# Splitting the move of a transposed attention tile between ScalarE and VectorE in the last five units of layer 1

## The reference

```python
proj = rmsnorm(x) @ b_w_in                        # queries: 36 dilated heads and 4 memory heads of 64
mix = dilated_mixture(rope(q_dil), shared_k, shared_v)   # 3 (window, dilation) groups, combined
mo = memory_attention(q_mem, mem_k, mem_v)        # 256 memory tokens
x = x + concatenate([mix, mo]) @ w_out
x = x + peer(rmsnorm(x), ...)                     # 16 experts for each of 8 heads and 512 tokens
```

## Time and profile before

| | us |
|---|---|
| median of 3 runs | 3196.49 (3196.42 to 3196.59) |
| the profiled execution, its own time | 3195.37 |
| its span in the trace | 3193.6 |
| TensorE busy | 3150.6 |
| VectorE busy | 2545.1 |
| ScalarE busy | 1636.8 |

### The profile page before, as it was taken

The page is one execution under the profiler, slowest core; times in us unless marked ns, Lnnn a source line. Parts: engine busy times, 40 slices in busy tenths (PEclk is TensorE's granted clock), DMA queues, the critical chain, the costliest instruction groups (busy, mean ns, idle before and its releaser), DMA issues.

```text
span 3193.6 us, 48756 instructions
## 1 busy us (share of the span) xinstructions
PE 3150.6 (99%) x17822; PEld 2817.2 (88%) x17822; DVE 2545.1 (80%) x5378; ACT 1636.8 (51%) x3053; POOL 1020.8 (32%) x626
## 2 busy tenths in 40 slices
PE   8999999999999999999999989999999999999999
PEld 7878899999998888888978868899999998888887
DVE  5685898989857988885378876898989866888886
ACT  5343249696943333335255654248686853333333
POOL 1001464545422444520000000354445432444440
PEclk9999999999999999999999999999999999999999
DMA  5123269898999999993222214259898998999994
GB/s 199 44 66 118 85 222 349 308 351 303 354 366 340 379 391 390 396 367 115 68 86 74 87 61 138 81 171 337 314 346 312 345 383 315 374 401 398 389 392 146
DMA packets 324925, 827.33 MB, mean 259 GB/s; under 512 B 26064, under 2 KB 158672, under 8 KB 317520
## 3 DMA queue, kind: packets, MB, share of 16 engines
q1 hardware_dynamic: 250960, 555.75, 48.5%
q0 software_dynamic: 73728, 268.47, 22.5%
HBM read 718.16 MB, written 105.96 MB: 258 GB/s over the span
## 4 chain that ended last, share of the span: by engine, by line
PE 43%; DVE 3%; DMA 2%; ACT 1%; issue 1%; SPq 0%; DVEq 0%; ACTq 0%
PE p_bank L2346 16%; PE p1r_h_ps L2282 16%; PE ba_bank L416 6%; PE o_bank L1753 1%; DMA hiddens<-p_h_sb 1%; PE p1r_gate_ps L2330 1%; PE ba_oT_ps L476 1%; PE ba_t_ps L497 1%; PE p1r_s_ps L2306 0%; PE ba_s_ps L439 0%; DVE p_grow L2711 0%; DVE ba_e L644 0%; ACT p1r_cols L2452 0%; PE ba_s_ps L444 0%; DMA raw<-in_u 0%
## 5 line engine op out<-in xcount | busy, mean ns | idle before, releaser
L2413 ACT ACTIVATE peer_hi<-raw 128x1024 fp32r<-128x1024 f32 x540 | 570.9, 1057 | 673.9 <-PE p_bank L2346 604.3
L2703 DVE TENSOR_TENSOR peer_lo<-raw,peer_hi 128x1024 fp32r<-128x1024 f32 x434 | 530.0, 1223 | 308.1 <-ACT peer_hi L2413 307.3
L2244 POOL TENSOR_TENSOR peer_lo<-raw,peer_hi 128x1024 fp32r<-128x1024 f32 x106 | 263.3, 2485 | 1083.2 <-ACT peer_hi L2413 1083.1
L2256 POOL DMA_INDIRECT p_grow<-in_v_rows,p_expert x256 | 388.6, 1518 | 468.9 <-DVE p_acc L2720 384.1
L2256 POOL DMA_INDIRECT p_grow<-in_u_rows,p_expert x256 | 359.2, 1403 | 506.8 <-DVE p_hid L2711 479.2
L2346 PE MATMUL p_bank<-peer_hi,p_w_hi 128*128 128x512 f32 x1500 | 461.8, 389 | 0.0
L2346 PE MATMUL p_bank<-peer_hi,p_w_lo 128*128 128x512 f32 x1500 | 461.8, 389 | 0.0
L2346 PE MATMUL p_bank<-peer_lo,p_w_hi 128*128 128x512 f32 x1500 | 461.7, 389 | 0.0
L2282 PE MATMUL p1r_h_ps<-h_hi,peer_hi 128*128 128x384 f32 (+2 forms) x1152 | 396.9, 345 | 1.3 <-ACT p_h_sb L2431 0.9
L2282 PE MATMUL p0r_h_ps<-h_hi,peer_hi 128*128 128x384 f32 (+2 forms) x1152 | 396.7, 344 | 0.6 <-DVE peer_lo L2703 0.5
L2282 PE MATMUL p1r_h_ps<-h_lo,peer_hi 128*128 128x384 f32 (+2 forms) x1152 | 391.4, 340 | 0.0
(11 more groups left out here) (438 smaller groups left out, 5531.9 us busy)
## 6 DMA issues: line engine op xcount, KB each, us to landing
raw<-in_u SPq DMA_DIRECT2D x256, 512.0 KB, 6.1
raw<-in_v SPq DMA_DIRECT2D x256, 512.0 KB, 8.3
p_g_sb<-gates SPq DMA_DIRECT2D x64, 768.0 KB, 11.1
hiddens<-p_h_sb SPq DMA_DIRECT2D x240, 192.0 KB, 4.7
p_w_raw<-hiddens SPq DMA_DIRECT2D x60, 768.0 KB, 7.5
gates<-x SPq DMA_DIRECT2D x24, 1024.0 KB, 9.7
raw<-in_w_b_mix SPq DMA_DIRECT2D x38, 512.0 KB, 3.5
raw<-in_w_peer_q SPq DMA_DIRECT2D x32, 512.0 KB, 3.6
```

Source lines behind the costliest of these rows:

```text
L2244: pool.tensor_tensor(lo[:, m % NH, :], raw[:, m % NR, :], hi[:, m % NH, :].bitcast(F32), ALU.subtract).then_inc(lo_pool, 1)
L2256: pool.indirect_dma_start(out=grow[:, g % RG, :], out_offset=None, in_=table, in_offset=bass.IndirectOffsetOnAxis(ap=expert[:, at:at + 1], ...
L2413: act.activation(hi[:, n % NH, :], raw[:, n % NR, :], ACT.Copy).then_inc(hi_ready, 1)
L2703: dve.tensor_tensor(lo[:, m % NH, :], raw[:, m % NR, :], hi[:, m % NH, :].bitcast(F32), ALU.subtract).then_inc(lo_dve, 1)
```

## The change

For the units after 22, that is 23 to 27, `move_turned` on ScalarE moves only the first bank of `t_ps` (128x512). A new function `move_other` on VectorE moves the second. VectorE issues it in step s = n + 1, behind `finish(s-4)` and ahead of `maximum(s+1)` and of what else the step holds. A new semaphore, `t_moved_too`, counts it. `output(n)` and `turn(n)` on TensorE wait for both semaphores.

```diff
@@ output(n), TensorE
                 pe.wait_ge(t_moved, n + 1)
+                if n > DENSE:
+                    pe.wait_ge(t_moved_too, n - DENSE)
@@ turn(n), TensorE
                     pe.wait_ge(t_moved, n)
+                    if n - 1 > DENSE:
+                        pe.wait_ge(t_moved_too, n - 1 - DENSE)
@@ move_turned(n), ScalarE
-                act.activation(eT[:, n % 2, :, :], t_ps[:, :, :], ACT.Copy).then_inc(t_moved, 1)
+                b = slice(0, 1 if n > DENSE else 2)
+                act.activation(eT[:, n % 2, b, :], t_ps[:, b, :], ACT.Copy).then_inc(t_moved, 1)
@@ new, VectorE
+            def move_other(n):
+                dve.wait_ge(turned, n + 1)
+                dve.wait_ge(valued, n - 1)
+                dve.tensor_copy(eT[:, n % 2, 1, :], t_ps[:, 1, :]).then_inc(t_moved_too, 1)
@@ the loop over steps, VectorE
+                if DENSE < s - 1 < UNITS:
+                    move_other(s - 1)
                 if DENSE < s + 1 < UNITS:
                     maximum(s + 1)
```

More of the change, by code:

```diff
@@ L340, in dilated_stage @@
         (hi_ready, lo_ready, summed, bank_free, shuffled, sin_ready, rot_done, scored, maxed, biased, exped, turned,
-         t_moved, valued, copied, returned, inverted, o_moved, near_stored, near_loaded, shifted, cexped, combined, own,
+         t_moved, t_moved_too, valued, copied, returned, inverted, o_moved, near_stored, near_loaded, shifted, cexped, combined, own,
          mem_k_loaded, mem_v_loaded) = [
             st.sem(s) for s in ("hi_ready", "lo_ready", "summed", "bank_free", "shuffled", "sin_ready", "rot_done",
-                                "scored", "maxed", "biased", "exped", "turned", "t_moved", "valued", "copied",
+                                "scored", "maxed", "biased", "exped", "turned", "t_moved", "t_moved_too", "valued", "copied",
                                 "returned", "inverted", "o_moved", "near_stored", "near_loaded", "shifted", "cexped", "combined", "own",
```

## The result

The changed kernel takes 3209.94 us at the median of 5 runs (3205.37 to 3214.97), against 3196.42 for the kernel before in the same comparison. The ratio is 1.0039, with a 95% interval of 1.0029 to 1.0050, so some 9 to 16 us are lost. The forecast was 3208.3, in a range of 3204.0 to 3212.5.

A forecast was written before the change was run, and what follows sets the result against it. TensorE, busy 3150.6 of 3193.6 us, was taken as the bound. Queue delay 8.25 plus clock falls 2.0 and 1.6 made 11.85 us, added to 3196.49 for 3208.3 us, range 3204 to 3212.5.

The forecast's parts named there:

- Unit 23: VectorE's half delays maximum(25) and finish(21) by 1.61 us, so turn_back(22) starts 0.86 late.
- Units 24 and 25: The loop from turn to turn takes 5.29 us instead of 4.67, making turn(26) 2.10 late.
- Step 27: VectorE's shift waits behind move_other(26); ScalarE's combine(4) comes 5.27 us late and output(26) 4.82 late.
- Step 28: Combination waits behind VectorE's last half; turn_back(26) 7.23 us late, the output projection's first product 8.25 late, kept to the end.
- The clock: TensorE's clock falls to 1.2 GHz at two new long gaps, costing 2.0 and 1.6 us.
- the first fall: Half clock behind the gap before output(26), slowing output(26), turn_back(25) and turn(27); 2.0 us.
- A: Rival of no loss: slack takes up VectorE's late start, only the shorter move counts; 3194.8 us, chance 0.06.
- B: Rival: the queue delays hold but no fall of the clock costs anything; 3204.7 us, chance 0.15.
- C: Rival: clock also falls in units 23 to 25, about 2.2 us more per affected period; 3210.5 to 3213, chance 0.15.
- D: Rival: shift(4) and combine(4) have slack, so only part of the chain holds; 3198.6 to 3202.5 us, chance 0.09.
- One sign: In the changed profile, turn_back in units 22 to 24 waits about 1.2 us each for the finish multiply.
- the second fall: Half clock from the gap before turn_back(26) into the first products; 0 to 3.1 us, middle 1.6 taken.

The follow-up runs named there:

- e3: Changed kernel with only units 26 and 27 split, units 23 to 25 moved by ScalarE alone; 3206.06 us, ratio 1.0031 to the kernel before.
- e4: Changed kernel with VectorE's shift and combination ahead of the halves of units 26 and 27, maxima still behind the halves; 3200.02 us, ratio 1.0008.
- e5: Changed kernel with 40 unread identity transposes filling TensorE's two long gaps; 3204.58 us, ratio 1.0026 to the kernel before.
- e7: The changed kernel run again unaltered, to see how far it repeats; 3208.61 us, ratio 1.0036 to the kernel before.
- e1: Changed kernel with VectorE's halves of units 23 to 27 each moved to the end of its step; 3198.87 us, ratio 1.000.
- e2: Changed kernel with only units 23 to 25 split, units 26 and 27 moved by ScalarE alone; 3201.34 us, ratio 1.0011 to the kernel before.

## Why the prediction was right, step by step

Counted from `turn(22)`, so less 3.40 against the rows of before:

- **Unit 23.** `turn_back(22)` 0.86 late predicted; 1908.93 - 1904.66 - 3.40 = 0.87 measured.
- **Units 24 and 25.** A period of 5.29 predicted, 5.25 measured (1910.34 to 1915.59). `turn(26)` 2.10 late predicted, 2.01 measured.
- **Step 27.** Shift at +5.27 by the sum (1918.04 against 1912.77), +5.20 measured. `output(26)` 4.82 late predicted, 4.77 measured. e3 and e4 show that it is the shift's place that does this.
- **Step 28.** Without the clock, the first product 8.25 late predicted; e5, which has no fall, measured 8.11. The last product is as late (8.12), so nothing was given back and the late loads of output weights cost nothing, as priced.
- **The clock.** I had 2.0 for the first fall, 1.6 for the second. The halves of unit 27 are 1928.66 - 1919.02 - 3.40 = 6.24 late, 1.42 more than the queue's 4.82: the fall came within `output(26)`, which so took 1.48 and not double. The second: 11.4 late at the last product against 9.6 at the first, 1.8. The sum, 3.2, stands for the 3.6 of the text. e3, where the first fall came before `output(26)`, has 1.98 and 1.91 for output and turn and is 1.9 above its 6.15 at the first product.
- **The rivals.** A is out: the wait of `turn_back` is there in every kernel with an early half. B is e5. C happened in one of the two profiles of the changed kernel and cost 1.6 there, against the 2.2 that I gave it. D is out, as the chain holds link for link. (D's upper end, 3202.5, doesn't follow from its own terms: 2.1 and half of the other 9.75 give 3203.5.)

One sign was a little off: `turn_back` was to wait about 1.2 us in each of units 22 to 24; it waited 1.07, 0.83 and 0.84. The sum doesn't use these waits, and its steps are right to 0.15. Part of the agreement is luck: 1.6 was the middle of an open range of 0 to 3.1 for the second fall, and the shares of the two falls changed from one profile of the same kernel to the next (1.4 and 1.8 in the first; in e7 the second gave 12.65 - 11.28 = 1.4, with 1.6 more for the fall in unit 24).

What the forecast didn't foresee is how far the kernel before varies: its three runs lay within 0.2 us, and later ones between 3190.3 and 3207.3. The median's 1.6 above the forecast is within that. So the medians alone couldn't confirm the terms of the sum; the distances in the profiles do.

## What to carry to other kernels

A faster operation can be a slower kernel when it is put into an in-order queue ahead of work that was ready earlier: ask of a moved or added instruction not only how long it takes but how long its engine will stand waiting to begin it (here up to 6.2 us for 0.7 us of work), and who waits for the instructions behind it. Where a producer fills two banks one after the other, start the consumer on the first as soon as it is full, on the same engine; here that won 1.4 us, where a second engine lost 1.2 even at the end of its steps (e1). And where single times vary by more than the effect, measure the distance between two landmarks on either side of the change in the profiles.

## What the runs showed of the hardware

In the first profile of the changed kernel TensorE's granted clock fell at gaps of 3.66 and 2.56 us, in e3 at gaps of 3.66 and 2.29. In e7 it fell at the first, of 3.65; behind the second, of 2.56, `turn_back(26)` (0.41) and `turn_o` (0.60) still ran at full speed, and it fell at the short gap after them, of 0.79. And once, in e7, it fell behind gaps of only 0.83 and 1.08 with 1.1 us of work between them. It did not fall at gaps of 1.93 (e2) and 1.50 (e4), nor at those of 2.11 (changed) and 2.17 (e2) in front of `turn_back(20)`. It stayed low for some 3 us behind the first gap and some 6 behind the second in the first profile, against the 6 and more of the two falls of the earlier trace rows. With idle transposes of 2.78 and 1.97 us in the two gaps it stayed up (e5). So whether the clock falls depends on more than the length of one gap, and each fall on the path cost another 0.7 (the second of e3, 8.82 - 8.09) to 1.9 us (its first, 8.09 - 6.15).

ScalarE reading one bank of a PSUM tile and VectorE the other at the same time slowed neither: 0.60 and 0.69 us side by side at 1905.97, as instructions of the same size take in the earlier trace rows. The Trainium skill ("PSUM — Partial Sum Buffer", section "Specifications (TRN2)") says as much of accesses to different banks, and this trace agrees.
